# Ring slots with a free semaphore each, and the last two expert pairs' rows kept on the core

## What is computed

```python
def modulation(cond, w_mod, b_mod):
    m = jax.nn.silu(cond) @ w_mod + b_mod
    return jnp.split(m[..., None, :], 6, axis=-1)
...
    hid = jax.nn.silu(jnp.einsum("nd,edf->nef", x, w_gate)) * jnp.einsum("nd,edf->nef", x, w_up)
    y = jnp.einsum("nef,efd->nd", hid * gates[:, :, None].astype(hid.dtype), w_down)
...
for l in range(DEPTH):
    ...
    xp = layer_norm(ALPHA * xp + mp[2] * op, ln_g[l, 0], ln_b[l, 0])
    hp = modulate(xp, mp[3], mp[4])
    fp = moe(hp, router_w, router_bias, exp_w_gate[l], exp_w_up[l], exp_w_down[l])
    xp = layer_norm(ALPHA * xp + mp[5] * fp, ln_g[l, 1], ln_b[l, 1])
```

## Time and profile before

| | us |
|---|---|
| median of 3 runs | 893.26 (889.69, 893.26, 897.0) |
| profiled execution | 890.76 |
| its span | 888.9 |
| TensorE matmul busy | 766.5 (86%) |
| TensorE weight load busy | 372.4 (42%) |
| VectorE busy | 299.2 (34%) |
| ScalarE busy | 146.6 (16%) |
| GpSimd busy | 58.8 (7%) |

### The profile page before, as it was taken

One profiled execution on the slowest core, in us unless ns is written; L12 is line 12 of the kernel. 1 busy time (PEld: TensorE's weight loads), 2 busy tenths in 40 slices (PEclk: granted clock), 3 DMA queues, 4 the chain that ended last, 5 costly groups with the idle time before them and its releaser, 6 DMA issues.

```text
span 888.9 us, 9820 instructions
## 1 busy us (share of the span) xinstructions
PE 766.5 (86%) x3695; PEld 372.4 (42%) x3695; DVE 299.2 (34%) x595; ACT 146.6 (16%) x386; POOL 58.8 (7%) x118
## 2 busy tenths in 40 slices
PE   3898888988999989889769967997799999978973
PEld 1355445454444334324234614554644434432431
DVE  0004444562322121211372063546422212121148
ACT  0211323221111011101120103323211111110110
POOL 0000000002000001000100030000200000100010
PEclk9698799998999999999989998997599999998997
DMA  8999922099999999999997099822079999999961
GB/s 314 367 342 401 388 80 87 9 387 407 416 427 423 420 423 426 423 417 428 402 376 272 11 373 426 348 95 94 1 285 423 424 421 422 425 425 415 426 278 48
DMA packets 69083, 288.39 MB, mean 324 GB/s; under 512 B 5004, under 2 KB 10636, under 8 KB 60852
## 3 DMA queue, kind: packets, MB, share of 16 engines
q1 hardware_dynamic: 64724, 275.59, 77.5%
q10 hardware_dynamic: 3168, 8.08, 2.3%
q0 software_dynamic: 1152, 4.19, 1.2%
HBM read 278.99 MB, written 8.86 MB: 324 GB/s over the span
## 4 chain that ended last, share of the span: by engine, by line
PE 50%; DMA 26%; DVE 12%; issue 8%; ACT 2%; POOL 1%; SPq 1%; DVEq 0%; POOLq 0%; ACTq 0%
DMA ring<-in_exp_w_up 19%; PE bank L966 14%; PE bank L716 8%; PE bank L803 5%; PE bank L1018 5%; DMA ring<-in_w_mod 5%; PE bank L650 4%; PE bank L751 3%; DMA ring<-expert_rows,spot_i 2%; PE bank L938 2%; PE bank L782 2%; PE bank L760 2%; PE bank L629 1%; DVE arena L1467 1%; ACT arena L1580 1%
## 5 line engine op out<-in xcount | busy, mean ns | idle before, releaser
L966 PE MATMUL bank<-ring,arena 128*64 128x512 f32 x1024 | 235.2, 616 | 25.5 <-DMA ring<-in_exp_w_up 24.8
L966 PEld LDWEIGHTS bank<-ring,arena 128*64 128x64 f32 x1024 | 79.9, 142 | 177.1 <-issue 177.0
L1018 PE MATMUL bank<-ring,arena 128*64 128x512 f32 x512 | 113.4, 595 | 3.8 <-DMA ring<-in_exp_w_down 3.8
L1465 DVE TENSOR_SCALAR arena<-arena 128x256 f32<-128x256 f32 x32 | 9.4, 294 | 257.6 <-ACT arena L1619 257.6
L716 PE MATMUL bank<-ring,arena 128*128 128x512 f32 (+2 forms) x224 | 75.5, 500 | 0.7 <-ACT arena L1553 0.7
L650 PE MATMUL bank<-ring,cwin 128*32 128x512 f32 x384 | 51.9, 689 | 20.4 <-DMA ring<-in_w_mod 20.4
L1543 ACT ACTIVATE arena<-bank 128x512 f32<-128x512 f32 (+6 forms) x79 | 40.4, 532 | 169.1 <-PE bank L716 67.4
L938 PE MATMUL bank<-arena 128*128 128x128 f32 x512 | 64.9, 283 | 3.0 <-POOL arena L1767 3.0
L1018 PEld LDWEIGHTS bank<-ring,arena 128*64 128x64 f32 x512 | 36.3, 137 | 69.1 <-issue 66.0
L938 PEld LDWEIGHTS bank<-arena 128*128 128x128 f32 x512 | 62.2, 199 | 4.0 <-POOL arena L1767 3.1
L803 PE MATMUL bank<-ring,arena 128*128 128x512 f32 x128 | 59.6, 599 | 0.0
(11 more groups left out here) (166 smaller groups left out, 613.9 us busy)
## 6 DMA issues: line engine op xcount, KB each, us to landing
ring<-in_exp_w_gate SPq DMA_DIRECT2D x32, 2048.0 KB, 26.6
ring<-in_exp_w_up SPq DMA_DIRECT2D x32, 2048.0 KB, 23.3
ring<-in_exp_w_down SPq DMA_DIRECT2D x32, 2048.0 KB, 31.2
ring<-in_w_mod SPq DMA_DIRECT2D x24, 2048.0 KB, 18.6
expert_rows<-arena ACTq DMA_DIRECT2D x14, 512.0 KB, 9.6
ring<-in_w_out_ab SPq DMA_DIRECT2D x2, 2048.0 KB, 16.5
ring<-in_w_in_c SPq DMA_DIRECT2D x2, 2048.0 KB, 30.7
ring<-in_w_out_c SPq DMA_DIRECT2D x2, 2048.0 KB, 19.8
```

Source lines behind the costliest of these rows:

```text
L966: mm = nc.tensor.matmul(pb(key)[SLOTS * hf:SLOTS * (hf + 1), :], xeT[b][:, k * P + SLOTS * a:k * P + SLOTS * (a + 1)], w[:, :, k, hf * 256 ...
L1018: mm = nc.tensor.matmul(pb(key)[SLOTS * a:SLOTS * (a + 1), :], hp[:, c:c + SLOTS], block_ap(n + 4 + a)[:, kf * D + hf * HALF: kf * D + (hf ...
```

## The change

- `blk_free` becomes nine semaphores, one per slot; a load waits for its own slot, and each block is given back by itself (`room_for`, `release`). Win block b - 1 is given back at the first product of win block b; gate and up at the first two products of the next gate/up; the last pair's downs at the end of TensorE's experts without waiting for VectorE; the back slot by VectorE when it has taken the rows.
- "back" stands in front of the last pair's six blocks in the ring's order.
- Rows of pairs 0 to 5 go by DRAM (`N_AWAY`); their gather waits for pair 5's store. Those of pairs 6 and 7 are both spread by products, four for each, in `last_pair`; the two add up in PSUM.
- In the last pair TensorE turns the one-hots of both pairs and broadcasts the gates between gate/up 0 and gate/up 1. VectorE takes the rows between the two halves' hidden.
- The store of a pair's rows is issued at the head of the next pair's ScalarE work instead of at the tail of its own. PSUM banks of gate/up, gathers, gates and spreads are dealt anew.

```diff
+def expert_blocks(l):
+    blocks = [("exp", l, b) for b in range(3 * N_EXP)]
+    return blocks[:-6] + [("back", l, 0)] + blocks[-6:]
...
+        def room_for(n):
+            return blk_free[n % RING], n // RING
+        def release(n):
+            return blk_free[n % RING], 1
...
-                    sp.wait_ge(blk_free, n - RING + 1)
+                    sp.wait_ge(*room_for(n))
...
+                            if b > 0 and (g, k) == (0, 0):
+                                mm.then_inc(*release(index[("win", l, b - 1)]))
...
-                        if free and (k, hf) == (0, 0):
-                            mm.then_inc(blk_free, 2)
+                        if k == 0 and used is not None:
+                            mm.then_inc(*release(used + hf))
...
+            def last_pair(l):
+                p, n = N_PAIR - 1, last_n[l]
+                for a in range(2):
+                    pe.wait_ge(*saved(("xe", l, a), p))
+                gate_up(l, 0, n, None, p, p % 3, n - 3)
+                turn_onehots(l)
+                gates(l, 1)
+                gate_up(l, 1, n + 2, None, p, p % 3, n)
+                hidden_turned(l, 0, p, n + 2)
+                pe.wait_ge(*saved(("ohT", l)))
+                for hf in range(2):
+                    pe.wait_ge(*saved(("ye", l, hf), p - 1))
+                    spread(l, hf, ye_sb, 0, False)
+                hidden_turned(l, 1, p, n + 3)
+                down(l, p, n + 4, None, (("ye_end", l), None))
+                for hf in range(2):
+                    pe.wait_ge(*(saved(("ye", l, 0), p) if hf == 0 else saved(("ye_end", l))))
+                    spread(l, hf, ye_end, 1, True)
+                for a in range(2):
+                    pe.sem_inc(blk_free[(n + 4 + a) % RING], 1)
...
-                pe.wait_ge(s_taken, l + 1)
-                pe.sem_inc(blk_free, 3)
...
+                dve.sem_inc(blk_free[back_n[l] % RING], 1)
...
-                both_hidden(l, N_PAIR - 1)
+                both_hidden(l, N_PAIR - 1, (0,))
                 rows_taken(l)
+                both_hidden(l, N_PAIR - 1, (1,))
...
-                pool.wait_ge(s_stored, 16 * (N_PAIR - 1) * (l + 1))
-                pool.wait_ge(blk_free, back_n[l] - RING + 1)
+                pool.wait_ge(s_stored, 16 * N_AWAY * (l + 1))
+                pool.wait_ge(*room_for(back_n[l]))
```

More of the change, by code:

```diff
@@ L100, in plan_blocks @@
     order += [("mod", 0, c) for c in MOD_PIECES[2]] + [("mod", 1, c) for c in MOD_PIECES[0]]
[L101 removed]
+    order += expert_blocks(0)
     order += [("win", 1, b) for b in range(len(WIN[1]))] + [("mod", 1, c) for p in (1, 2) for c in MOD_PIECES[p]]
     order += [("wout", 1, b) for b in range(2)]
[L104 removed]
+    order += expert_blocks(1)
     return order
@@ L608, in _ @@
             overflow(0)
-            for n in range(back_n[0] + 1, exp_n[1]):
+            for n in range(last_n[0] + 6, exp_n[1]):
                 load_block(n)
@@ L636, in ln_row, with modulation @@
                 bcast(key, cst(C_ID + LN_ROW + 8 * which + 2 * (2 * l + s) + hf, 1), rows[:])
-            def modulation(l, piece, free=0):
+            def modulation(l, piece, used=()):
                 key = ("mod", l, piece)
@@ L932, in route, with gather @@
                     modulation(1, 0)
-            def gather(out, onehot, chunks, width):
+            def gather(out, onehot, chunks, width, used=None):
                 for i, k in enumerate(chunks):
@@ L940, in gather @@
                                               start=(g == 0), stop=(g == 1))
+                        if used is not None and (i, g) == (0, 0):
+                            mm.then_inc(*release(used))
                 return mm
@@ new lines, in spread @@
+            def spread(l, hf, pair_rows, which, done):
+                for g in range(G):
+                    key = ("y", l, 1, g, hf)
+                    if which == 0:
+                        room(pe, key)
+                    c = which * 256 + g * P
+                    mm = nc.tensor.matmul(pb(key)[:], ohT[:, c:c + P], pair_rows[:, hf * HALF:(hf + 1) * HALF],
+                                          start=(which == 0), stop=(which == 1), skip_group_check=True)
+                    if done:
+                        mm.then_inc(*fill(key))
@@ L1116, in _ @@
                 project(l)
-                modulation(l, 1, free=len(WIN[l]))
+                modulation(l, 1, (index[("win", l, len(WIN[l]) - 1)],))
                 if l == 1:
@@ L1473, in hidden, with both_hidden @@
                 V.tensor_tensor(hid, t_sb, gu[:, 256:512], ALU.mult).then_inc(*done)
-            def both_hidden(l, p):
-                for a in range(2):
+            def both_hidden(l, p, halves=(0, 1)):
+                for a in halves:
                     dve.wait_ge(s_ge, p * 2 + (N_EXP * l + a + 1))
```

202 lines of the change are left out of this document (97 added, 105 removed).

## The result

Seven runs of the changed kernel beside seven of the kernel before: 885.5 us median (880.8 to 889.2) against 892.0 (889.7 to 897.0); the ratio is 0.9932, interval 0.9903 to 0.9961. That is 6.5 us less by the medians.

What follows compares the result with a forecast made beforehand. DMA was taken to bound both expert sections, and the unloaded stretch from 485 to 509 us to make layer 1's modulation wait. Terms: -8.7 - 0.9 + 1.5 + 0.4 = -7.7 us, forecast 884 us, range 875 to 891.

Steps and rivals of the forecast that it cites:

- The ring: Layer 1's first modulation: win blocks freed early, no waits for weights, first scores at 531.2 instead of 539.93, -8.7 us.
- The release times: Layer 1's project: win blocks free, and three remaining loads issued, 13.7, 27.4 and 34.3 us after project's start.
- Where the gather goes: Last pair: gather issued at 395.4, landed at 410.7, its 2.1 MB in front of pair 7's gate and up.
- before 415: Sign that the forecast is right: the last pair's gather lands before 415 us.
- the taking leaves the tail for nothing: Rival, layer ends: pair 7's first weights come as early as now, sums 4.5 and 3.6 us earlier; about 875; chance 0.20.
- The path of 23.7 us to the downs and 8.1 from there to the sum: Last pair: downs start 23.7 us after pair 7's first up lands, the layer's sum 8.1 us behind them.
- Layer 0's end: Layer 0's sum starts at 451.5 instead of 452.45, -0.9 us, plus 1.5 for a clock drop behind a wait.
- Layer 1's end: Layer 1's sum starts at 871.9 instead of 871.53, +0.4 us, with the clock counted as 0.
- nearest to 2.68: Layer 1, before pair 7's first gate/up: a 3.0 us wait, likened to one of 2.68 without slowdown, clock counted 0.
- the last pair costs more than I count: Rival, last pair: clock falls in both layers and pair 6's first down waits, 6 us lost; about 890; chance 0.19.
- The sum, -7.7, 884: Whole kernel: modulation and both layer ends together save 7.7 us, giving 884 us; chance of 880 to 888 was 0.50.

Runs made afterwards that it cites:

- E3: The changed kernel with VectorE's taking of the rows behind both halves' hidden instead of between them; 885.4 us, ratio 0.9938.
- E6: The changed kernel without the gather, so the rows of pairs 0 to 5 are left out of the result; 874.0 us, ratio 0.9772.
- E2: The changed kernel with all win blocks given back only at the modulation behind project, as before; 892.2 us, ratio 1.0014.
- E1: The kernel before with a free semaphore per slot and early release of win blocks, old last pair kept; 884.4 us, ratio 0.9917.
- E4: E3 with the gather also held back until pair 7's first up has landed; 878.4 us, ratio 0.9862.
- E9: The changed kernel with unread products in TensorE's waits, three before pair 7's first gate/up, two in layer 1's query turning; 882.1 us, ratio 0.9912.
- E10: E4 with unread products in TensorE's waits, three ahead of pair 7's downs, two in the query turning; 874.0 us, ratio 0.9839.
- E7: The changed kernel with unread products in TensorE's waits, six before pair 7's first gate/up, five in layer 1's query turning; 888.5 us, ratio 0.9956.
- E5: The changed kernel with only the gather held back until pair 7's first up has landed, the taking left in place; 893.5 us, ratio 1.0010.
- E8: E4 with unread products in TensorE's waits, six ahead of pair 7's downs, five in the query turning; 882.9 us, ratio 0.9880.

## Why the prediction held, point by point

*The ring, -8.7 us: right.* Scores 65.5 us behind project's start were forecast; in the five kernels whose waits weren't filled and whose win blocks are freed early with the new last pair (after, E3 to E6) it is 64.3 to 66.9, mean 65.8. What ends the section is VectorE's last normalised row, as forecast; E2 takes the gain away, E1 gives it alone. What moves it between 64.3 and 66.9 is the clock, which the forecast didn't count: in E4 project took 43.43 us (granted 0.56 at its start) and the turning to the scores 4.10 (0.50), in the changed kernel 42.16 (0.84) and 2.81 (0.87). So the profiled 10.0 us hold 1.3 of a faster project, and with project as slow as before the gain is 7.2 to 7.6 (E1, E3, E4, E6); that the mean lies so near the forecast is partly luck. The release times were worked out too early (a third of 43.47 is 14.5, not 13.7): the three loads were issued 15.5, 28.8 and 35.7 us after project's start. No product waited for them.

*Where the gather goes: right in its cost, wrong in its landing.* It was forecast to be issued at 395.4 and to land at 410.7; it was issued from 397.6 on and landed at 421.5, 24 us later instead of 15, so the sign "before 415" failed. The 15.35 us were those of the gather in its old place; here it landed only 2 us ahead of pair 7's first up, beside whose loads it ran. There was slack enough, 14 us instead of 19, and nothing waited for it. It takes its bytes from pair 7's weights and costs 4.85 us there (E6), so the rival "the taking leaves the tail for nothing" was wrong.

*The path of 23.7 us to the downs and 8.1 from there to the sum: right,* 23.9 and 8.2 in E2, E6 and E9. In series as told: half 1's hidden behind the taking. (TensorE's own path adds up to 21.8, not 21.9; VectorE's decides.)

*Layer 0's end, -0.9 and 1.5 for the clock, together +0.6: nearly.* +1.2 in the profile, with 1.7 for the clock; -0.3 in E2 without it, where pair 7's first up came 25.2 us behind the anchor, 0.4 late, and the path took 0.2 more.

*Layer 1's end, +0.4: wrong in size.* It was +3.0. Two of its terms were too small. The clock was counted as 0, "nearest to 2.68"; the wait was 3.57 and the product took 8.78, 1.7 more. And pair 7's first up came 25.6 us behind the anchor instead of five blocks, 24.85, another 0.7; pair 6's downs had waited for their weights too (2.84). The rival "the last pair costs more than I count" had both; some 3 us of its 6 came true. Counted so, the sum is -8.5 + 1.2 + 3.0 = -4.3, less than the medians' -6.5. With the ends of E2, -0.3 and +2.7, it is -6.1, and by the ratios of E1 and E2 the ring is -7.4 and the last pair +1.3, together -6.1 too. How often the last pair is as dear as in the profiled execution, two profiles can't tell.

*The sum, -7.7, 884: the median is 885.5.* The forecast's mechanism held; the size that failed is that of layer 1's end, and it is larger than the 1.2 us by which the sum is off. The number came nearer than its terms did, in runs that scatter by 4 us on either side. The rework of the last pair shows no gain until the gather is moved too (E4).

## What to carry to other kernels

Give a ring's slots back where each block's last product has run, not where the stage ends: win blocks given back at the next block's first product put loads into a stretch of 24 us that had none, and took away the waits behind it (7.4 us in E1); the same semaphores raised at the stage's end did nothing (E2). The gather cost its bytes in a section where DMA was full, so ask which product's weights stand behind it: it cost 4.85 us in front of the weights with which the last path begins, and some 1 us where TensorE had its own work for that long (ends of 53.5 and 53.6 in E10, which also has the taking last, 52.5 without a gather). And work moved out of the tail helps only if what it is moved in front of isn't on the same path.

## What was not expected of the hardware

How often the clock falls behind a short wait. In the last two pairs of each layer of these twelve profiles, gate/up and down products behind a wait of 1.1 to 2.25 us took 7.09 in all 26 cases; behind 2.63 to 4.12 us, 23 of 28 took 8.4 to 10.1. Two waits of 3.41 in layer 0 (E2, E3) cost nothing, a third of 3.41 in layer 1 (E9) cost 1.4 and one of 2.63 cost 1.7: the length alone doesn't decide. Behind the filled waits of E7 to E10 all eight such products took 7.09. The Trainium skill (TensorE: Matmul & The Clock Gate, Part 1) says that an idle array falls to half its clock, and that the place where it switches back to the full one varies from run to run. The rows agree on the first, with 0.50 granted behind the 2.63 us wait. To count such a wait as free because one of its length once was, as I did for layer 1, was the mistake; 23 of 28 at some 1.7 us each, an estimate from these cases, would have been 1.4.

The run-to-run spread goes with the same clock. In 65 runs of the kernel before, beside the experiments, those of 888 us or less had a mean granted clock of 0.927 to 0.939 over the run, those of 895 or more 0.916 to 0.924. In the profiles too: the anchor in layer 0 is reached at 396.8 or later where the clock up to there was 0.92 or 0.93 (after, E5, E8), and earlier where it was 0.94 or 0.95 (all others). What decides whether the clock falls behind one wait and not behind another of the same length stays open.
